# State update of a chunked gated delta rule: write strength and decay applied to the values instead of the keys

## The reference, cut to what matters

```python
k_tail = k * jnp.exp(gc[..., -1:] - gc)[..., None]
g_tot = jnp.exp(gc[..., -1])

def step(s, inp):
    u_n, w_n, qk_n, qd_n, kt_n, gt_n = inp
    v_new = u_n - jnp.einsum("bhck,bhkv->bhcv", w_n, s)
    o = jnp.einsum("bhck,bhkv->bhcv", qd_n, s) + jnp.einsum("bhcj,bhjv->bhcv", qk_n, v_new)
    s = s * gt_n[..., None, None] + jnp.einsum("bhck,bhcv->bhkv", kt_n, v_new)
    return s, o
```

## Time and profile before

| | |
|---|---|
| median of 3 runs | 3098.97 us (3089.36 to 3110.85) |
| profiled execution | 3085.82 us, span 3083.8 us |
| PE busy | 2696.4 us (87% of the span), PEld 2584.0 |
| DVE busy | 1753.1 us (57%) |
| ACT busy | 1236.6 us (40%) |
| POOL busy | 1166.7 us (38%) |
| mean granted TensorE clock | 0.941 |

### The profile page before, as it was taken

The page is one execution under the profiler, slowest core; times in us unless marked ns, Lnnn a source line. Parts: engine busy times, 40 slices in busy tenths (PEclk is TensorE's granted clock), DMA queues, the critical chain, the costliest instruction groups (busy, mean ns, idle before and its releaser), DMA issues. The chain is left out here.

```text
span 3083.8 us, 53025 instructions
## 1 busy us (share of the span) xinstructions
PE 2696.4 (87%) x18741; PEld 2584.0 (84%) x18741; DVE 1753.1 (57%) x2671; ACT 1236.6 (40%) x2107; POOL 1166.7 (38%) x1110
## 2 busy tenths in 40 slices
PE   4799999985997389999999799999999999986994
PEld 3799999975995289999999689998998999975993
DVE  3266666665102357787777656766766767654004
ACT  2255555554102234444444334554544545542001
POOL 3333333322220134445444354544554555433220
PEclk9899999997998699999999889999999999997996
DMA  3111111112324035555554352424324243214214
GB/s 113 50 54 55 60 55 55 55 42 97 111 68 173 14 99 145 148 150 157 150 157 143 113 155 44 116 48 106 90 65 107 47 117 108 47 29 166 76 39 174
DMA packets 249410, 292.57 MB, mean 95 GB/s; under 512 B 87419, under 2 KB 210892, under 8 KB 247580
## 3 DMA queue, kind: packets, MB, share of 16 engines
q1 hardware_dynamic: 244636, 273.35, 30.7%
q10 hardware_dynamic: 4608, 17.04, 1.7%
HBM read 194.30 MB, written 96.05 MB: 94 GB/s over the span
## 5 line engine op out<-in xcount | busy, mean ns | idle before, releaser
L1897 ACT ACTIVATE zz<-ps 104x416 fp32r<-104x416 f32 x560 | 287.1, 519 | 375.8 <-PE ps L1788 374.6
L553 PE MATMUL ps<-dn_yhi,dn_whi 128*128 128x416 f32 (+1 forms) x1152 | 395.3, 343 | 18.5 <-POOL dn_wlo L537 13.1
L1960 DVE TENSOR_TENSOR pp<-ps,level_mask 104x416 fp32r<-104x416 f32 x560 | 319.2, 588 | 117.8 <-PE ps L1788 117.2
L554 PE MATMUL ps<-dn_ylo,dn_whi 128*128 128x416 f32 (+1 forms) x1152 | 375.9, 326 | 0.0
L555 PE MATMUL ps<-dn_yhi,dn_wlo 128*128 128x416 f32 (+1 forms) x1152 | 375.8, 326 | 0.0
L553 PE MATMUL ps<-rg_yhi,rg_whi 128*128 128x416 f32 (+1 forms) x768 | 257.2, 335 | 57.9 <-POOL rg_wlo L537 37.1
L1790 PE MATMUL ps<-pp,zz 104*104 104x208 f32 x1440 | 264.8, 294 | 18.2 <-DVE pp L1960 15.9
L554 PE MATMUL ps<-rg_ylo,rg_whi 128*128 128x416 f32 (+1 forms) x768 | 256.4, 334 | 0.0
L555 PE MATMUL ps<-rg_yhi,rg_wlo 128*128 128x416 f32 (+1 forms) x768 | 255.0, 332 | 0.0
L1790 PE MATMUL ps<-zz,pp 104*104 104x208 f32 x1440 | 245.5, 280 | 0.0
L553 PEld LDWEIGHTS ps<-dn_yhi,dn_whi 128*128 128x128 f32 x1152 | 218.7, 190 | 24.9 <-POOL dn_wlo L537 13.5
(11 more groups left out here) (276 smaller groups left out, 7385.6 us busy)
## 6 DMA issues: line engine op xcount, KB each, us to landing
c_nq<-nq_scratch SPq DMA_DIRECT2D x160, 169.0 KB
dn_raw<-in_dn_w_in SPq DMA_DIRECT2D x48, 512.0 KB, 4.1
qd<-rows_scratch SPq DMA_DIRECT2D x160, 104.0 KB, 3.2
rg_raw<-in_rg_w_in SPq DMA_DIRECT2D x32, 512.0 KB, 4.0
nq_scratch<-p_nq SPq DMA_DIRECT2D x48, 338.0 KB
p_ex<-rows_scratch SPq DMA_DIRECT2D x32, 422.5 KB
nq_scratch<-p_rn SPq DMA_DIRECT2D x32, 338.0 KB
o_scratch<-a SPq DMA_DIRECT2D x16, 520.0 KB, 2.8
```

Of the source, the lines that this page charges most:

```text
L553: e.matmul(o, whi, mhi[:, t0:t0 + tn], start=(first and k == 0), stop=False)
L554: e.matmul(o, whi, mlo[:, t0:t0 + tn], start=False, stop=False)
L1897: e.activation(zz[:, b, :, :], ps[0:CH, 2 * b + 1, 0:m4], ACT.Copy).then_inc(zev.sem, 1)
L1960: e.tensor_tensor(D4(pp[:, b, l % 2, :, :]), D4(Y4), c["level_mask"][:, l, :, 0:CH].unsqueeze(2).to_broadcast([CH, 2, 2, CH]), ALU.mult).t ...
```

## The change

- GpSimd no longer makes `kt`; the buffer and its semaphore `kt_done` are gone.
- ScalarE, after its four copies into `vn`, makes four more of the same bank into a new buffer `vt` with the scale `head["tail"]`. That table now holds tail times beta (VectorE makes it with one multiplication in place of a copy, once a head).
- TensorE's state product takes the keys as loaded (`krow`) as the stationary operand and `vt` as the moving one: for each direction one product of 256 columns, in place of two of 128. It now comes after the outputs in piece 2.
- VectorE in piece 2 takes the outputs first and then updates the state.
- The wait for the loaded key rows moves from GpSimd to TensorE; SyncE's `load` and VectorE's `tables` lose or exchange the wait on `kt_done`.

```diff
@@ dn_chunks, load (SyncE)
                 if h >= 2:
                     e.wait_ge(om.sem, om.at(n, (h - 2) * NC + NC))
-                    e.wait_ge(kt_done.sem, kt_done.at(n, (h - 2) * NC + NC))
                     e.wait_ge(gated.sem, gated.at(n, (h - 2) * 5 + 5))
@@ state (GpSimd)
-                        e.wait_ge(krow_in[i].sem, krow_in[i].at(n, 16 * (g // STEPS + 1)))
...
                     ins.then_inc(qd_done.sem, 1)
-                    if g >= 2 and (g - 2) % NC != NC - 1:
-                        e.wait_ge(sm.sem, sm.at(n, inner(g - 2, False)))
-                    for d in range(2):
-                        ins = e.tensor_tensor(kt[:, b, 2 * d:2 * d + 2, :],
-                                              krow[:, i, chunk(g, d), :].unsqueeze(1).to_broadcast([CH, 2, P]),
-                                              head["tail"][:, i, d, g % NC, :].unsqueeze(2).to_broadcast([CH, 2, P]),
-                                              ALU.mult)
-                    ins.then_inc(kt_done.sem, 1)
@@ state, piece 2 (TensorE)
                         e.wait_ge(vn_done.sem, vn_done.at(n, g + 1))
-                        e.wait_ge(kt_done.sem, kt_done.at(n, g + 1))
-                        if not final:
-                            for m in range(4):
-                                ins = e.matmul(ps[:, 7, m * P:(m + 1) * P], kt[:, b, m, :], vn[:, m, :],
-                                               start=True, stop=True)
-                            ins.then_inc(sm.sem, 1)
                         e.wait_ge(qd_done.sem, qd_done.at(n, g + 1))
...
                         ins.then_inc(om.sem, 1)
+                        e.wait_ge(vt_done.sem, vt_done.at(n, g + 1))
+                        if not final:
+                            if first:
+                                e.wait_ge(krow_in[i].sem, krow_in[i].at(n, 16 * (g // STEPS + 1)))
+                            for d in range(2):
+                                ins = e.matmul(ps[:, 7, d * 2 * P:(d + 1) * 2 * P], krow[:, i, chunk(g, d), :],
+                                               vt[:, 2 * d:2 * d + 2, :], start=True, stop=True)
+                            ins.then_inc(sm.sem, 1)
@@ state, piece 1 (ScalarE)
                         ins.then_inc(vn_done.sem, 1)
+                        for m in range(4):
+                            ins = e.activation(vt[:, m, :], ps[0:CH, 7, m * P:(m + 1) * P], ACT.Copy,
+                                               scale=head["tail"][:, i, m // 2, g % NC, m % 2:m % 2 + 1])
+                        ins.then_inc(vt_done.sem, 1)
@@ tables (VectorE)
-                    e.wait_ge(kt_done.sem, kt_done.at(n, (h - 2) * NC + NC))
+                    e.wait_ge(vt_done.sem, vt_done.at(n, (h - 2) * NC + NC))
...
+                    elif name == "tail":
+                        ins = e.tensor_tensor(head[name][:, i], src, tabs["beta"][:, :, :, bass.ds(n * 4 + 2 * h, 2)],
+                                              ALU.mult)
@@ state, piece 2 (VectorE): the block from om to oacc is moved ahead of the block from sm to snew
+                        e.wait_ge(om.sem, om.at(n, g + 1))
...
+                            e.tensor_tensor(dst, dst, src, ALU.add).then_inc(oacc.sem, 1)
                         if k < NC - 1:
                             e.wait_ge(sm.sem, sm.at(n, inner(g, False)))
...
                             ins.then_inc(snew.sem, 1)
-                        e.wait_ge(om.sem, om.at(n, g + 1))
...
-                            e.tensor_tensor(dst, dst, src, ALU.add).then_inc(oacc.sem, 1)
```

More of the change, by code:

```diff
@@ L1554, in dn_chunks @@
         pp = sb(s, "pp", [CH, 2, 2, 4, CH], F32R)
-        qd, kt, st = sb(s, "qd", [P, 2, 4, CH]), sb(s, "kt", [CH, 2, 4, P]), sb(s, "st", [P, 2, 4, P])
+        qd, vt, st = sb(s, "qd", [P, 2, 4, CH]), sb(s, "vt", [CH, 4, P]), sb(s, "st", [P, 2, 4, P])
         rr, vn = sb(s, "rr", [CH, 4, P]), sb(s, "vn", [CH, 4, P])
@@ L1569, in dn_chunks @@
         u_done, tb_done = each("u"), each("tb")
-        qd_done, kt_done, vm, vn_done, om, oacc = (each(x) for x in ("qd", "kt", "vm", "vn", "om", "oacc"))
+        qd_done, vt_done, vm, vn_done, om, oacc = (each(x) for x in ("qd", "vt", "vm", "vn", "om", "oacc"))
         ksm, r_done, sm, snew = (S(x, 2 * (NC - 1)) for x in ("ksm", "r", "sm", "snew"))
@@ L1986, in state @@
                     elif piece == 2:
+                        e.wait_ge(om.sem, om.at(n, g + 1))
+                        src = ps[:, 6, 0:m4].rearrange("p (d r i) -> p d r i", d=2, r=2)
+                        dst = both(g, vo[:, i].rearrange("p r (k i) -> p k r i", i=CH))
+                        if k == 0:
+                            e.wait_ge(o_out[i].sem, o_out[i].at(n, 16 * (g // STEPS)))
+                        if k < PAIRS:
+                            e.tensor_copy(dst, src).then_inc(oacc.sem, 1)
+                        else:
+                            e.wait_ge(oacc.sem, oacc.at(n, g))
+                            e.tensor_tensor(dst, dst, src, ALU.add).then_inc(oacc.sem, 1)
                         if k < NC - 1:
```

## The result

The changed kernel takes **3128.28 us** (median of 4 runs, 3125.84 to 3130.5) against 3096.07 us of the kernel before (4 runs, 3089.36 to 3110.85). The ratio is 1.0097, 95% interval 1.0059 to 1.0136: **slower by 1.0%**. The interval lies above 1, so the loss is small but clear. The profiled execution has a span of 3125.8 us, 42 us more than before. That of before was 10 us faster than this median, so the profiles show more than the medians do.

A forecast was written before the change was run, and what follows sets the result against it. TensorE was taken to set the pace in the chunk stage, stalling on VectorE's pp. Eight heads at 2.24 us (17.9) plus 7x0.92 (6.4) gave +24 on 3099, 3123 us; range for 8 of 10: 3086 to 3145.

The forecast's parts named there:

- Rival 1: VectorE's tail of state updates is hidden after all, leaving only TensorE's own work: 3080 us, chance 0.15.
- Odd steps: Steps 1, 3, 5, 7 of a head: VectorE's state updates delay pp and TensorE's next level, +0.45 us each.
- Even steps of first halves: Steps 2 and 4 of a head: VectorE's tail delays pp and TensorE's slot 5, +0.28 us each.
- Even steps of second halves: Steps 6 and 8 of a head: ScalarE's squares start early and stop delaying zz, -0.06 us each.
- Step 0: First step of a head: second ScalarE copy delays previous head's logarithm and zz, +0.92 us, for 7 heads.
- The matmuls: TensorE's state product: two 256-column products replace four of 128, 0.19 us less a step, 13.7 us where TensorE sets time.
- The sum: All steps together: 17.9 us over eight heads plus 6.4 us for the logarithm's delay, +24 us.
- The decay table becomes a product, 8 times, 0.: VectorE's per-head tables: a product of two 40-column tables, once in each of 8 heads, costs 0.
- Rival 2: Longer TensorE gaps at table steps and turn starts make the clock fall more often: +14 to +41 us, chance 0.13.
- rival 3: Merged state matmuls save nothing and their result comes 0.2 us later: 3136 us, chance 0.12.
- Rival 4: Second ScalarE copy not hidden in ordinary steps, 40 even steps up to 1 us late: +40 us at most, chance 0.05.
- GpSimd's relief: GpSimd's key scaling, 94.9 us busy that nobody waited for, goes away: worth 0.

The follow-up runs named there:

- e1: Kernel before with only the order changed (outputs first, state product last, VectorE's state update after taking the outputs): 3132.5 us, ratio 1.010.
- e10: Kernel before with its table copies on ScalarE and the new order (outputs first, state product and update last): 3108.4 us, ratio 1.0051.
- e7: Changed kernel with the state product first again, vt made ahead of vn, state updated before the outputs are taken: 3106.7 us, ratio 1.0025.
- e6: Changed kernel without the second ScalarE copy, the state product reading vn: 3123.3 us, ratio 1.0093.
- e2: Kernel before with only the state product changed, to two 256-column products of loaded keys by vn, in the old place: 3093.9 us, ratio 0.9989.
- e3: Changed kernel with three of the four per-head table copies (gt, beta, eg) made by ScalarE: 3108.7 us, ratio 1.0033.
- e4: Kernel before with all four per-head table copies made by ScalarE: 3079.6 us, ratio 0.9935.
- e9: Changed kernel with VectorE's four table copies moved from the period's start to after slot 6: 3100.3 us, ratio 1.0035.

## Why the prediction was right, and where its terms were off

*The direction and the mechanism.* The forecast was 3123 us, +24 us, with outputs first as the cause; measured were 3128.3 us and +32 us. The cause is shown by itself in e1 and e10, and e7 takes it away again. The time came 3 us closer than the change, since the median of the kernel before, 3099.0 in the forecast, is 3096.1 with its fourth run. Rival 1 (the tail is hidden) is out: every odd step and every even step of a first half has the tail in its distance, whole or less the slack there was.

*Odd steps, +0.45 forecast.* Measured +0.52 to 0.53. The outputs took 1.80 us behind another group instead of 1.71, and the rest of the chain was as read.

*Even steps of first halves, +0.28 forecast.* Measured +0.45. The outputs behind an inverse group take 1.83 us (2269.18 to 2271.01), and from `pp` to TensorE it was 0.72 us there, not 0.64.

*Even steps of second halves, -0.06 forecast.* Measured +0.03 to +0.11, for the same reason. That the squares stop mattering was right.

*Step 0, +0.92 forecast.* Measured +0.77, and e6 shows that it is the second copy. The logarithm is 0.98 us later, as worked out, but `zz` begins 0.55 us after it (2190.20 to 2190.75) and not 0.71 as in the earlier trace rows.

*The matmuls, -0.19 a step forecast.* 0.03 or 0.14, by place (e2). The new group itself came out as read, 0.70 us against the 0.74 taken, because in the changed kernel an inverse follows it as in the earlier trace rows. What I left out is that its neighbours change with the place. The outputs, now behind an inverse group, take 1.80 us instead of 1.71, and the old group of eight takes 0.83 us in the new place (e1, 2285.91 to 2286.74), not 0.93. It hardly counted, since the steps wait for VectorE.

*The sum.* 32 x 0.53 + 16 x 0.45 + 16 x 0.07 + 7 x 0.77 = 30.7 us against 24. The two profiles differ by 44 us between the first and the last piece 2 (1001.7 against 957.8). The other 13 us lie around the table copies. From the piece 2 of step 3 to that of step 4 the eight heads together take 12.0 us more, of which the tail is 4.2; behind it, in two heads, the clock is still low during step 4 (16.0 and 15.9 us where 13.0 is usual), some 6 us. The median distance of step 3 grew by 1.44 us instead of 0.53, but at two of the turns' starts it shrank (7.00 to 6.14, 10.20 to 9.53), so over all seven table steps the distances hold only 2 us more than the tail, and most of the rest goes with 24 us more at 1.2 GHz.

The medians give the same picture from another side. With the tables on ScalarE in both kernels (e3 against e4) the change costs 29.1 us, with them on VectorE 32, so of the loss at most a few microseconds belong to the table steps: the held copies cost the kernel before nearly as much as the changed one.

*"The decay table becomes a product, 8 times, 0."* This term was put at 0 without a look at those instructions, and in the profile it failed: the table step grew by 0.9 us more than the tail, 5.96 to 7.40. Not the product but the copies beside it came to lie under a GpSimd instruction (e1 has no product and 7.42 us). I had read the gap at 1850.47 in the earlier trace rows only as a wait for `pp`. VectorE's rows ahead of it, in the kernel before, would have told (start, duration):

```profile
1847.88 0.91 DVE L1949 COPY head_tail<-tail 104x40 f32 x1
1848.70 0.17 DVE L1949 COPY head_gt<-gt 128x40 f32 x1
1848.79 0.17 DVE L1949 COPY head_beta<-beta 104x40 f32 x1
...
1848.88 1.04 DVE L1947 TENSOR_SCALAR head_eg<-eg 104x40 f32 x1
```

Two of the four take 0.91 and 1.04 us there where the others take 0.17. That is 1.6 us of VectorE in front of `pp`, and e4 shows that it was worth taking away.

*Rival 2 (the clock falls more often), 0.13.* Partly true in the profile: six of the seven table steps are followed by a fall of the clock instead of three, and four of the six (1975.5, 2234.9, 2490.9, 2617.2) stand where it had stayed full. That was a sign of being wrong that the prediction named, and it came. In the medians the difference is 32 us, no more than the ordinary steps hold, so how much of it the falls make up from run to run stays open. The held copy had more part in it than the tail, as far as one profile of each kernel can say: e3 and e9 keep the tail with the copies free and have two falls, but e10 has four.

*Rivals 3 and 4.* The merged group saves next to nothing in the old place (0.03 us, e2) and 0.13 us in the new one, so rival 3 was half right, without the result coming late: VectorE starts on it 1.09 us after the group begins (2284.25 to 2285.34), as read. Rival 4, the second copy late in every even step, is out by e6.

*GpSimd's relief, 0.* Right: e1 keeps that work and is no slower than the changed kernel beyond their intervals.

## What to carry to other kernels

Where a step ends on one engine and the next begins with what another must still deliver, look at the queue of the delivering engine: what stands under a longer piece of work counts nothing, what stands last in a piece counts in all that goes beyond the slack there. Swapping two pieces of equal total work moved a microsecond of updates from cover to tail. It cost 0.5 us in most steps and only 0.03 to 0.11 where ScalarE had been late anyway, 1% in all. Moving 95 us of work off an engine that nobody waits for gains nothing, and small copies between SBUF tiles belong where GpSimd is quiet, or on ScalarE.

## What the runs showed of the hardware

A VectorE copy of 104x40 fp32 within SBUF takes 0.18 us, or until GpSimd's running instruction ends (up to 1.10 us), and some hundredths of a microsecond in the order of starts decide it. Once, in e1 at 1848.88, `eg` was held through three GpSimd instructions that followed each other without a gap, 2.21 us. On ScalarE the same copies took 0.22 to 0.29 us beside GpSimd's instructions, and nothing was held. VectorE's operations that read PSUM kept their 0.59 us beside GpSimd's work. The Trainium skill (SBUF — State Buffer, section SBUF: two separate sides) states the rule: of a GpSimd operation and a VectorE operation that is in a two-port mode, or has two inputs in SBUF while GpSimd's reads SBUF, "whichever" starts first has the shared ports "for the whole instruction". The rows agree with it: 1.07 us for the held copy, ended with GpSimd's instruction, and 0.87 us for the product of two SBUF tables at 2102.44 of the changed kernel. The 2.21 us in e1 go beyond it, since the waiting instruction was passed over by GpSimd's next two. And the starts in the profile do not give the order away: at 2218.03 before, GpSimd's instruction starts 0.02 us ahead of the beta copy and is the one that takes longer, while in e1, at 2234.08, it starts 0.02 us ahead too and the copy is held (1.08 us).

Four matmul instructions of 256 columns (two fp32 products) hold TensorE 0.70 us before an inverse group, whose weights are 104 columns of fp32r, and 0.90 us before the outputs, whose weights are 128 columns of fp32. Eight of 128 columns hold it 0.83 and 0.93 us in the same two places. Whether the width or the type of the neighbour's weights makes the difference, no run separates.

The granted clock did not follow the length of TensorE's idle gaps alone. Most falls to 1.2 GHz came behind gaps of 1.6 to 3.4 us, but two gaps of 2.2 us (e4, at its turn starts) went without one, and four of 0.9 to 1.0 us (one in e3, one in e6, two in e10) were followed by one, while five of 0.9 us in e9 were not. The same stage spent between 7 and 72 us at that level, and with the few gaps of these profiles what decides between them stays open.
